# Banded attention of a diffusion backbone: the masks added by TensorE as identity times mask, and the softmax bias taken from a minimum over negated raw scores

## The chip, the cores and the metric

The kernel runs on one core of a Trainium2 chip. The metric is the device time of one execution in microseconds (us), the median of the runs shown. The engines are named as in the profile: PE is TensorE (its weight loads are listed apart as PEld), DVE is VectorE, ACT is ScalarE, POOL is GpSimd, SP is SyncE.

## The reference, cut to what matters

The program is a two-layer backbone over 512 latent tokens and 256 context tokens with 1024 channels. Only one stage of it is changed in its inner loop: the attention of the odd layer. 16 query heads of 64 channels share 4 key heads. A latent query sees all context keys, the latent keys within 128 positions, and one learned logit per head (the sink), all in one softmax:

```python
band = jnp.abs(qi[:, None] + WINDOW - kj[None, :]) <= WINDOW
...
s_loc = jnp.einsum("bqhrd,bkhd->bhrqk", qb, kb).astype(F32) * scale
s_loc = jnp.where(valid, s_loc, -jnp.inf)
s_ctx = jnp.einsum("bqhrd,bkhd->bhrqk", qb, kc).astype(F32) * scale
prob = jax.nn.softmax(jnp.concatenate([s_loc, s_ctx, sink_l], axis=-1), axis=-1).astype(v.dtype)
```

The queries are normalised (root mean square, times a gain vector `q_g`) and rotated before this; `scale` is 1/8.

## The kernel before, in words

The stage works through 32 units: 8 pairs of heads times 4 query tiles of 128 rows. A unit holds two heads (`e` is 0 or 1) whose 64 channels lie in the lower and the upper half of the partitions, so that the score matmuls of the two heads use the upper and the lower 64 rows of the PE array. A unit at either end of the sequence (query tile 0 or 3, an *outer* unit) has 4 key tiles of 128 per head: 2 of context, 2 of its neighbourhood. A unit in the middle (query tile 1 or 2, an *inner* unit) has 5. One key tile per head of an outer unit, and two per head of an inner one, lie on the edge of the band and need a triangular mask. The scores of unit u lie in three of the eight banks of PSUM (the accumulation memory); even and odd units take different banks. Head 0 of an inner unit takes columns 0 to 639 and head 1 columns 896 to 1535, so that key tile (head 0, number 4) and key tile (head 1, number 0) share a bank; the semaphore `wn_tail` makes the matmul of tile (1,0) wait until that of tile (0,4) is done.

Nothing is scheduled by a planner: each engine has its own program, written out as one loop over u, and works it in order.

- PE (`pe_window`), for u: the scores of unit u (L1428, after the exponentials of unit u-2); then the transposes of the probabilities of unit u-2 (L1446), in rounds of up to four tiles through one bank (2 rounds for an outer unit, 3 for an inner one), each round after ACT has copied out the one before; between and behind the rounds the products with the values of unit u-3 (L1470). I call these blocks S, T and V.
- ACT (`act_window`), for u: the copies of the rounds of unit u-2 (L1485); the rounded output of unit u-3 (L1489); then the exponentials of unit u, one for each head with its row sum (L1498), and of the sink (L1502).
- DVE (`dve_window`), for u: mask added in PSUM (L1512), maximum over each head's scores (L1517), then small ones of 128x2: maximum with the sink (L1520), the negated maximum as bias (L1523), sink minus maximum (L1524). Then the sum, reciprocal and normalisation of unit u-1 (L1530 to L1535), and the rest of the output of unit u-3 (L1541).

The two ends of the stage meet the neighbouring products: the value projection (L1204) ahead, the output projection (L498) behind, whose first products are already mixed into the last units. POOL works far from this stage, above all at the start of the program, where it issues loads of modulation weights (L669, L692).

Of the kernel before, what the change touches and what calls it, by code (L numbers as in the profile page):

```python
# [16 lines left out]
F32R = mybir.dt.float32r  # L17

ACT = mybir.ActivationFunctionType
ALU = mybir.AluOpType  # L20
# [30 lines left out]
C_ID, C_ONE, C_BLK, C_UF, C_UB, C_TF, C_TB, C_MP, C_MN, C_SW, C_COS, C_SIN = (  # L51
    0, 128, 256, 384, 512, 640, 768, 896, 1024, 1152, 1280, 1792)
C_ALL = 2304
NEG = -1.0e30


VA_MOD, VA_C, VA_CC, VA_N = 0, 72, 80, 88
# [5 lines left out]
def shape_constants():  # L63

    c = np.zeros((P, C_ALL), np.float32)
    i = np.arange(P)
    c[:, C_ID:C_ID + P] = np.eye(P)
    c[:, C_ONE:C_ONE + P] = 1.0
    c[:, C_BLK:C_BLK + P] = (i[:, None] // 64) == (i[None, :] // 64)
    c[:, C_UF:C_UF + P] = i[:, None] > i[None, :]  # L70
    c[:, C_UB:C_UB + P] = i[:, None] < i[None, :]
    c[:, C_TF:C_TF + P] = i[:, None] <= i[None, :]
    c[:, C_TB:C_TB + P] = i[:, None] >= i[None, :]
    c[:, C_MP:C_MP + P] = np.where(i[None, :] >= i[:, None], 0.0, NEG)
    c[:, C_MN:C_MN + P] = np.where(i[None, :] <= i[:, None], 0.0, NEG)
    swap = np.zeros((P, P), np.float32)
    for o in range(P):
        j = o % 32
        if j < 16:
            swap[o + 16, o] = -1.0  # L80
        else:
            swap[o - 16, o] = 1.0
    c[:, C_SW:C_SW + P] = swap
    quarter = 16
    freqs = (np.float32(10000.0) ** (-np.arange(quarter, dtype=np.float32) / np.float32(quarter))).astype(np.float32)
    t = np.arange(SEQ)
# [34 lines left out]
def build(nc, a, out):  # L121
# [5 lines left out]
    with ExitStack() as ctx:  # L127
# [102 lines left out]
        sink = sb("sink", QH)  # L230
        stat = sb("stat", 32)
        gst = sb("gst", 64)

        def blocks_(x, t=T):
            return x[:, :].rearrange("p (b t) -> p b t", t=t)
# [18 lines left out]
        def c_(at, n=P):  # L254
# [50 lines left out]
        v_mm, v_done, v_done_act = sem("v_mm"), sem("v_done"), sem("v_done_act")  # L305
        at_sc, at_m0, at_nm, at_ex, at_ri, at_pn, at_tr, at_pt, at_pv, at_o = (
            sem("at_" + s) for s in ("sc", "m0", "nm", "ex", "ri", "pn", "tr", "pt", "pv", "o"))
        kk_two, wn_tail = sem("kk_two"), sem("wn_tail")
        wn_sc, wn_mk, wn_mx, wn_m, wn_nm, wn_sk, wn_ex, wn_es, wn_l, wn_ri, wn_n0, wn_n1, wn_tr, wn_pt, wn_pv, wn_hi, wn_lo = (
            sem("wn_" + s) for s in ("sc", "mk", "mx", "m", "nm", "sk", "ex", "es", "l", "ri", "n0", "n1", "tr", "pt", "pv",  # L310
                                     "hi", "lo"))
        pj_ev = sem("pj_ev")
        cv_pad, cv_tap, cv_out = sem("cv_pad"), sem("cv_tap"), sem("cv_out")
# [1057 lines left out]
        for x in range(8):  # L1371
            for qt in range(SEQ // P):
                lo, hi = max(0, qt - 1), min(3, qt + 1)
                if hi - lo == 2:
                    tiles = ([4, 5, qt - 1, qt + 1, qt], [qt, 4, 5, qt - 1, qt + 1])
                    order = [(0, 4, 1), (1, 1, 2), (0, 0, 2), (1, 3, 1), (0, 2, 1), (1, 4, 1), (0, 3, 1), (1, 0, 1)]
                    first, mask = (0, 896), (256, C_MP, 256)
                else:
                    tiles = ([4, 5, lo, hi], [4, 5, lo, hi])
                    order = [(0, 0, 2), (1, 0, 2), (0, 2, 2), (1, 2, 2)]  # L1380
                    first, mask = (0, 1024), ((384, C_MN, P) if qt == 0 else (256, C_MP, P))
                WU.append(dict(x=x, g=x // 2, q0=P * qt, tiles=tiles, order=order, first=first, mask=mask, n=P * len(tiles[0])))
        NWU = len(WU)
        rounds = tails = 0
        for x in WU:
# [4 lines left out]

        def win(u, c0, c1):
            return ps[:, 1536 * (u % 2) + c0:1536 * (u % 2) + c1]

        def pool_keys(pool):

# [16 lines left out]
                    mm.then_inc(w_used, 1)  # L1412

        def pe_window(pe):
            early = [(d, k) for k in range(DB - 1) for d in range(2)]
            for u in range(NWU + 3):
                if u < NWU:
                    x = WU[u]
                    g, q0 = x["g"], x["q0"]
                    if u >= 2:  # L1420
                        pe.wait_ge(wn_ex, 2 * u - 2)
                    for e, j, m in x["order"]:
                        c = x["first"][e] + P * j
                        k0 = P * x["tiles"][e][j]
                        r = slice(64 * e, 64 * e + 64)
                        if x["tail"] and (e, j) == (1, 0):
                            pe.wait_ge(wn_tail, x["tail"])
                        mm = pe.matmul(win(u, c, c + P * m), gq[r, x["x"], q0:q0 + P], gk[r, g, k0:k0 + P * m],  # L1428
                                       start=True, stop=True)
                        if x["tail"] and (e, j) == (0, 4):  # L1430
                            mm.then_inc(wn_tail, 1)
                    mm.then_inc(wn_sc, 1)
                todo = list(range(WU[u - 3]["n"] // P)) if u >= 3 else []
                i = u - 2
                if 0 <= i < NWU:
                    x = WU[i]
                    nt = 2 * x["n"] // P
                    for r in range(x["nr"]):
                        if r == 0:
                            pe.wait_ge(wn_n0, i + 1)  # L1440
                        if 4 * r + 4 > nt // 2 and (r == 0 or 4 * r <= nt // 2):
                            pe.wait_ge(wn_n1, i + 1)
                        if x["r0"] + r:
                            pe.wait_ge(wn_pt, x["r0"] + r)
                        for k in range(4 * r, min(nt, 4 * r + 4)):
                            mm = pe.transpose(bank(6)[:, P * (k % 4):P * (k % 4) + P], gp[:, i % 3, P * k:P * k + P], ident)  # L1446
                        mm.then_inc(wn_tr, 1)
# [27 lines left out]
        def act_window(act):  # L1475
            for u in range(NWU + 3):
# [13 lines left out]
                if u < NWU:  # L1490
# [5 lines left out]
                    for e in range(2):  # L1496
                        c = x["first"][e]
                        act.activation(gp[:, u % 3, n * e:n * e + n], win(u, c, c + n), ACT.Exp,  # L1498
                                       bias=gst[:, u % 4, 2, e:e + 1], scale=HD ** -0.5,
                                       accum_out=gst[:, u % 4, 4, e:e + 1]).then_inc(wn_ex, 1)  # L1500
                    act.wait_ge(wn_sk, u + 1)
                    act.activation(gst[:, u % 4, 5, :], gst[:, u % 4, 3, :], ACT.Exp).then_inc(wn_es, 1)  # L1502

        def dve_window(dve):
            for u in range(NWU + 3):
                if u < NWU:
                    x = WU[u]
                    f = gst[:, u % 4]
                    dve.wait_ge(wn_sc, u + 1)
                    c0, mk, w = x["mask"]  # L1510
                    s = win(u, 0, 1536).rearrange("p (b n) -> p b n", n=512)[:, 0:3:2, c0:c0 + w]
                    dve.tensor_tensor(s, c_(mk, w).rearrange("p (o n) -> p o n", o=1).broadcast_to([P, 2, w]), s,  # L1512
                                      ALU.add).then_inc(wn_mk, 1)
                    dve.wait_ge(wn_mk, u + 1)
                    c = x["first"][1]
                    s = win(u, 0, 2 * c).rearrange("p (b n) -> p b n", n=c)[:, :, 0:x["n"]]
                    dve.tensor_reduce(f[:, 0, :], s, AX, ALU.max).then_inc(wn_mx, 1)  # L1517
                    sk = sink[:, 2 * x["x"]:2 * x["x"] + 2]
                    dve.wait_ge(wn_mx, u + 1)
                    dve.scalar_tensor_tensor(out=f[:, 1, :], in0=f[:, 0, :], scalar=HD ** -0.5, in1=sk,  # L1520
                                             op0=ALU.mult, op1=ALU.max).then_inc(wn_m, 1)
                    dve.wait_ge(wn_m, u + 1)
                    dve.tensor_scalar(f[:, 2, :], f[:, 1, :], -1.0, None, ALU.mult).then_inc(wn_nm, 1)  # L1523
                    dve.tensor_tensor(f[:, 3, :], sk, f[:, 1, :], ALU.subtract).then_inc(wn_sk, 1)  # L1524
                i = u - 1
                if 0 <= i < NWU:
                    f, n = gst[:, i % 4], WU[i]["n"]
# [1222 lines left out]
        def _(act):  # L2750
# [59 lines left out]
            act_norm(act, 3)  # L2810
            act_s_ff(act, 2)
            act_norm(act, 4)
            act_items(act, n_even, len(items), BASE["odd"])
            act_split(act, BASE["out", R_GQA])
            act_v_o(act)
# [95 lines left out]
```

## Time and profile before

| what | value |
|---|---|
| median of 3 runs | 3269.77 us (3262.24 to 3270.68) |
| span of the profiled execution | 3264.5 us |
| PE busy | 3099.5 us, 95% |
| DVE busy | 1924.2 us, 59% |
| ACT busy | 1137.1 us, 35% |
| the attention stage, first scores to last value product | 2693.6 to 2843.7 us |

The profiled execution's span stands for its time; no time of its own is listed beside it, and it lies between the lowest run and the median. Times of day in the rows are microseconds from the start of the span. A busy share of PE counts overlapping matmuls once, so it says when PE had something in flight, not how much of its rate was used.

### The profile page before, as it was taken

The page shows a single profiled execution, that of the slowest core. Times are in us where ns is not written, and L with a number is a line of the kernel's source. Part 1 is how long each engine was busy: PE and PEld are TensorE (multiplying, and loading weights), DVE is VectorE, ACT ScalarE, POOL GpSimd, SP SyncE. Part 2 cuts the span into 40 slices and gives each one's busy share as a digit, 9 for nine tenths or more (in the row PEclk, how much of TensorE's full clock was granted, in tenths as well). Part 3 has the DMA queues.
Part 4 walks back from the last instruction along what each step waited for, and adds up shares of the span by engine and source line. Part 5 has one row for each costly group of instructions (what it writes and reads, how often), then busy time and mean ns, then how long its engine had stood idle before and what let it go on. Part 6 is the DMA issues. An engine that isn't in the chain of part 4 may idle for free.

```text
span 3264.5 us, 43658 instructions
## 1 busy us (share of the span) xinstructions
PE 3099.5 (95%) x17735; PEld 2739.4 (84%) x17735; DVE 1924.2 (59%) x2675; ACT 1137.1 (35%) x1750; POOL 266.0 (8%) x317
## 2 busy tenths in 40 slices
PE   4999999999999998899999999999999998999999
PEld 4999999987669895488999988999998876678887
DVE  7754536424552535767778765877778448643333
ACT  5211212456441321235323334533323536642222
POOL 1100000200001005620000001000000100000000
PEclk8999999999999999999999999999999999999999
DMA  5533424411004220012343321333333120023332
GB/s 205 172 104 104 128 72 137 123 40 52 7 1 124 64 65 14 1 33 78 110 129 104 117 65 59 112 99 106 104 117 118 50 59 8 14 84 97 97 97 90
DMA packets 314303, 274.19 MB, mean 84 GB/s; under 512 B 17426, under 2 KB 290057, under 8 KB 313865
## 3 DMA queue, kind: packets, MB, share of 16 engines
q1 hardware_dynamic: 286992, 182.35, 18.7%
q0 software_dynamic: 25488, 89.14, 8.7%
q8 instruction: 130, 2.13, 0.3%
q14 instruction: 52, 0.43, 0.0%
q10 hardware_dynamic: 1641, 0.14, 0.0%
HBM read 263.21 MB, written 8.39 MB: 83 GB/s over the span
## 4 chain that ended last, share of the span: by engine, by line
PE 52%; DVE 3%; ACT 2%; issue 1%; POOL 0%; ACTq 0%; DVEq 0%
PE ps L2229 30%; PE ps L498 16%; PE ps L1446 1%; ACT gpt L1485 1%; DVE hs_lo L2422 1%; ACT gp L1498 1%; PE ps L1470 1%; PE ps L1428 1%; PE ps L1204 1%; PE ps L2311 0%; DVE vw_lo L2162 0%; PE ps L1884 0%; DVE h_sb L2430 0%; PE ps L1901 0%; DVE ms_s L2453 0%
## 5 line engine op out<-in xcount | busy, mean ns | idle before, releaser
L488 DVE TENSOR_TENSOR w_lo<-ring,w_hi 128x1024 fp32r<-128x1024 f32 (+3 forms) x221 | 251.3, 1138 | 452.4 <-ACT w_hi L473 363.5
L498 PE MATMUL ps<-u_hi,w_hi 128*128 128x384 f32 (+2 forms) x1584 | 468.5, 355 | 22.1 <-DVE u_lo L659 18.0
L498 PE MATMUL ps<-u_hi,w_lo 128*128 128x384 f32 (+2 forms) x1584 | 462.1, 351 | 0.0
L498 PE MATMUL ps<-u_lo,w_hi 128*128 128x384 f32 (+2 forms) x1584 | 462.0, 351 | 0.0
L473 ACT CAST w_hi<-ring 128x1024 fp32r<-128x1024 f32 (+3 forms) x157 | 149.4, 952 | 613.4 <-PE ps L498 574.4
L498 PEld LDWEIGHTS ps<-u_hi,w_hi 128*128 128x128 f32 x1584 | 285.6, 190 | 48.1 <-issue 25.6
L498 PEld LDWEIGHTS ps<-u_lo,w_hi 128*128 128x128 f32 x1584 | 286.7, 190 | 22.7 <-issue 1.7
L498 PEld LDWEIGHTS ps<-u_hi,w_lo 128*128 128x128 f32 x1584 | 285.6, 189 | 21.2
L2156 ACT CAST vw_hi<-ring 128x1024 fp32r<-128x1024 f32 (+1 forms) x176 | 181.2, 1030 | 341.9 <-PE ps L2229 280.7
L2162 DVE TENSOR_TENSOR vw_lo<-ring,vw_hi 128x1024 fp32r<-128x1024 f32 (+1 forms) x176 | 210.9, 1200 | 150.5 <-ACT vw_hi L2156 150.2
L2229 PE MATMUL ps<-u_hi,vw_hi 128*128 128x384 f32 x768 | 248.6, 337 | 12.8 <-DVE u_lo L659 12.3
L2229 PE MATMUL ps<-u_lo,vw_hi 128*128 128x384 f32 x768 | 248.0, 337 | 0.0
L2229 PE MATMUL ps<-u_hi,vw_lo 128*128 128x384 f32 x768 | 247.7, 336 | 0.0
L2229 PE MATMUL ps<-hs_hi,vw_hi 128*128 128x512 f32 x704 | 184.3, 343 | 15.7 <-DVE hs_lo L2422 8.0
L2229 PE MATMUL ps<-hs_hi,vw_lo 128*128 128x512 f32 x704 | 182.7, 341 | 0.0
L2229 PE MATMUL ps<-hs_lo,vw_hi 128*128 128x512 f32 x704 | 181.8, 339 | 0.0
L2229 PE MATMUL ps<-vv_hi,vw_hi 128*128 128x384 f32 x480 | 161.9, 337 | 0.0
L2453 DVE SCALAR_TENSOR_TENSOR ms_s<-cst,sc,ms_s 128x1024 f32<-128x1024 f32 x126 | 158.4, 1280 | 5.1 <-DVE ms_s L2453 0.5
L2229 PE MATMUL ps<-vv_hi,vw_lo 128*128 128x384 f32 x480 | 161.2, 336 | 0.0
L2229 PE MATMUL ps<-vv_lo,vw_hi 128*128 128x384 f32 x480 | 161.1, 336 | 0.0
L498 PE MATMUL ps<-hid_hi,w_hi 128*128 128x384 f32 (+1 forms) x528 | 159.5, 356 | 0.0
L498 PE MATMUL ps<-hid_hi,w_lo 128*128 128x384 f32 (+1 forms) x528 | 159.1, 355 | 0.0
(351 smaller groups left out, 5871.3 us busy)
## 6 DMA issues: line engine op xcount, KB each, us to landing
ring<-in_w_ff_in SPq DMA_DIRECT2D x176, 512.0 KB, 3.9
ring<-in_w_ff_out SPq DMA_DIRECT2D x72, 512.0 KB, 4.0
cst<-in_w_mod POOLq DMA_DIRECT2D x72, 512.0 KB, 3.9
m_in<-in_w_mod POOLq DMA_DIRECT2D x56, 512.0 KB, 4.0
ring<-in_w_in_e SPq DMA_DIRECT2D x26, 512.0 KB, 3.9
m_first<-in_w_mod POOLq DMA_DIRECT2D x16, 512.0 KB, 13.9
ring<-in_w_out_e SPq DMA_DIRECT2D x16, 512.0 KB, 3.8
ring<-in_w_ff_out SPq DMA_DIRECT2D x16, 384.0 KB, 3.4
```

The lines of the kernel that those rows point to most:

```text
L473: act.copy(w_hi[:, (n % 2) * SLOT:(n % 2) * SLOT + WIDE[n]], ring[:, (n % RING) * SLOT:(n % RING) * SLOT + WIDE[n]]).then_inc(w_split_hi, 1)
L488: dve.tensor_tensor(w_lo[:, b:b + WIDE[n]], ring[:, s:s + WIDE[n]], w_hi[:, b:b + WIDE[n]], ALU.subtract).then_inc(w_split_lo, 1)
L498: mm = pe.matmul(ps_at(p, c0, c1) if halved else pair(p)[:, c0:c1], w, x[:, c0:c1], start=start and i == 0, stop=stop and i == 2)
L1204: mm = pe.matmul(out, x, w[:, b:b + m], start=start and i == 0, stop=stop and i == 2)
L1428: mm = pe.matmul(win(u, c, c + P * m), gq[r, x["x"], q0:q0 + P], gk[r, g, k0:k0 + P * m], start=True, stop=True)
L1446: mm = pe.transpose(bank(6)[:, P * (k % 4):P * (k % 4) + P], gp[:, i % 3, P * k:P * k + P], ident)
L1470: mm = pe.matmul(bank(7)[64 * e:64 * e + 64, 0:P], gv[:, k, HD * y["g"]:HD * y["g"] + HD], gpt[:, u % 2, c:c + P], start=j == 0, stop=j == ...
L1485: act.copy(gpt[:, i % 2, c0:c1], bank(6)[:, 0:c1 - c0]).then_inc(wn_pt, 1)
L2156: act.copy(v_hi_w[c % 3][:, 0:src.shape[-1]], src).then_inc(c_hi, 1)
L2162: dve.tensor_tensor(v_lo_w[c % 3][:, 0:n], src, v_hi_w[c % 3][:, 0:n], ALU.subtract).then_inc(c_lo, 1)
L2229: mm = pe.matmul(y, w, x[:, c0:c1], start=start and i == 0, stop=stop and i == 2, skip_group_check=onto)
L2453: y = dve.scalar_tensor_tensor(out=at_, in0=w, scalar=by, in1=at_, op0=ALU.mult, op1=ALU.add)
```

## The change

Four edits belong together. The scale of 1/8 and a minus sign are multiplied into the gain vector of the query norm, and the sink is negated, both once, early, by POOL; the scores then come out of PE as minus the scaled logits. The masks hold plus 1e30 in place of minus 1e30 and are no longer added by DVE: two matmuls of PE per unit (128x128 identity times two blocks of 128 mask columns, one of them all zeros for an outer unit) write them into PSUM ahead of the scores, and the score matmuls of those key tiles add to them. The order of the score matmuls of a unit is changed, so that the masked tiles come first; for an inner unit this puts tile (0,4) next to last and tile (1,0) last. DVE takes a minimum where it took a maximum, and the minimum with the negated sink is the bias itself; the exponential runs with scale -1.

```diff
-                    order = [(0, 4, 1), (1, 1, 2), (0, 0, 2), (1, 3, 1), (0, 2, 1), (1, 4, 1), (0, 3, 1), (1, 0, 1)]
-                    first, mask = (0, 896), (256, C_MP, 256)
+                    order = [(0, 2, 1), (1, 3, 1), (0, 3, 1), (1, 4, 1), (0, 0, 2), (1, 1, 2), (0, 4, 1), (1, 0, 1)]
+                    first, masked, mask = (0, 896), ((2, 3), (3, 4)), wm[:, P:4 * P].rearrange("p (b n) -> p b n", n=P)[:, 0:3:2, :]
...
-                    order = [(0, 0, 2), (1, 0, 2), (0, 2, 2), (1, 2, 2)]
+                    order = [(0, 2, 2), (1, 2, 2), (0, 0, 2), (1, 0, 2)]
...
+        def pool_masks(pool):
+
+            pool.wait_ge(const_in, 16)
+            pool.tensor_copy(wm[:, 0:P], ident).then_inc(wm_made, 1)
+            pool.tensor_copy(wm[:, P:2 * P], c_(C_MP)).then_inc(wm_made, 1)
+            pool.tensor_scalar(wm[:, 2 * P:3 * P], ident, 0.0, None, ALU.mult).then_inc(wm_made, 1)
+            pool.tensor_copy(wm[:, 3 * P:4 * P], c_(C_MN)).then_inc(wm_made, 1)
+            pool.wait_ge(vec_done, 3)
+            pool.tensor_scalar(sink[:, :], sink[:, :], -1.0, None, ALU.mult).then_inc(turned, 1)
+            pool.tensor_scalar(vb[:, VB_GQ:VB_GQ + 1], vb[:, VB_GQ:VB_GQ + 1], -HD ** -0.5, None, ALU.mult).then_inc(turned, 1)
...
+            pe.wait_ge(wm_made, 4)
...
+                    for e in range(2):
+                        c = 1024 * e + 256
+                        pe.matmul(win(u, c, c + 256).rearrange("p (b n) -> p b n", n=P), wm[:, 0:P], x["mask"],
+                                  start=True, stop=False, skip_group_check=True)
...
-                                       start=True, stop=True)
+                                       start=j not in x["masked"][e], stop=True, skip_group_check=True)
...
-                                       bias=gst[:, u % 4, 2, e:e + 1], scale=HD ** -0.5,
+                                       bias=gst[:, u % 4, 2, e:e + 1], scale=-1.0,
...
+            dve.wait_ge(turned, 2)
...
-                    dve.tensor_tensor(s, c_(mk, w).rearrange("p (o n) -> p o n", o=1).broadcast_to([P, 2, w]), s,
-                                      ALU.add).then_inc(wn_mk, 1)
-                    dve.wait_ge(wn_mk, u + 1)
...
-                    dve.tensor_reduce(f[:, 0, :], s, AX, ALU.max).then_inc(wn_mx, 1)
+                    dve.tensor_reduce(f[:, 0, :], s, AX, ALU.min).then_inc(wn_mx, 1)
...
-                    dve.scalar_tensor_tensor(out=f[:, 1, :], in0=f[:, 0, :], scalar=HD ** -0.5, in1=sk,
-                                             op0=ALU.mult, op1=ALU.max).then_inc(wn_m, 1)
-                    dve.wait_ge(wn_m, u + 1)
-                    dve.tensor_scalar(f[:, 2, :], f[:, 1, :], -1.0, None, ALU.mult).then_inc(wn_nm, 1)
-                    dve.tensor_tensor(f[:, 3, :], sk, f[:, 1, :], ALU.subtract).then_inc(wn_sk, 1)
+                    dve.tensor_tensor(f[:, 2, :], f[:, 0, :], sk, ALU.min).then_inc(wn_nm, 1)
+                    dve.wait_ge(wn_nm, u + 1)
+                    dve.tensor_tensor(f[:, 3, :], f[:, 2, :], sk, ALU.subtract).then_inc(wn_sk, 1)
```

ACT also gets a wait for `turned` ahead of the odd layer's projections, and `pool_masks` stands between POOL's first loads (L669) and its next (L692).

On PE, around the scores of one inner unit, before: the last value product of an earlier unit, then six groups of score matmuls (`gk` keys, `gq` queries, `ps` PSUM), then the first transposes (`gp` probabilities, `cst` the identity).

```order
L1470 MATMUL ps<-gpt,gv 64x128 x2
L1428 MATMUL ps<-gk,gq 128x128 [waits wn_ex]
L1428 MATMUL ps<-gk,gq 128x256 x2
L1428 MATMUL ps<-gk,gq 128x128 x4
L1428 MATMUL ps<-gk,gq 128x128 [waits wn_tail]
L1446 MATMUL ps<-cst,gp 128x128 [waits wn_pt,wn_n0]
L1446 MATMUL ps<-cst,gp 128x128 x3
```

The first score row there is tile (0,4), seven matmuls ahead of the one that waits for it. The same place after the change, with the two mask matmuls (`wm`):

```order
L1489 MATMUL ps<-gpt,gv 64x128 x2
L1439 MATMUL ps<-wm 128x256 [waits wn_ex]
L1439 MATMUL ps<-wm 128x256
L1447 MATMUL ps<-gk,gq 128x128 x4
L1447 MATMUL ps<-gk,gq 128x256 x2
L1447 MATMUL ps<-gk,gq 128x128
L1447 MATMUL ps<-gk,gq 128x128 [waits wn_tail]
L1465 MATMUL ps<-cst,gp 128x128 [waits wn_pt,wn_n0]
L1465 MATMUL ps<-cst,gp 128x128 x3
```

The two mask matmuls stand between the value products and the scores and take over the wait for the exponentials, and the matmul that waits for `wn_tail` now directly follows the one that signals it. On DVE, one unit before (`gst` holds the small vectors):

```order
L1512 TENSOR_TENSOR ps<-cst,ps 128x2x128 [waits wn_sc]
L1517 TENSOR_REDUCE gst<-ps 128x2 [waits wn_mk]
L1520 SCALAR_TENSOR_TENSOR gst<-gst,sink 128x2 [waits wn_mx]
L1523 TENSOR_SCALAR gst<-gst 128x2 [waits wn_m]
L1524 TENSOR_TENSOR gst<-sink,gst 128x2
L1530 TENSOR_TENSOR gst<-gst 128x2 [waits wn_es,wn_ex]
L1532 RECIPROCAL gst<-gst 128x2 [waits wn_l]
L1534 TENSOR_SCALAR gp<-gp,gst 128x640 [waits wn_ri]
L1535 TENSOR_SCALAR gp<-gp,gst 128x640
L1541 TENSOR_TENSOR go_lo<-ps,go_hi 128x128 [waits wn_hi]
```

And after:

```order
L1532 TENSOR_REDUCE gst<-ps 128x2 [waits wn_sc]
L1535 TENSOR_TENSOR gst<-gst,sink 128x2 [waits wn_mx]
L1537 TENSOR_TENSOR gst<-gst,sink 128x2 [waits wn_nm]
L1543 TENSOR_TENSOR gst<-gst 128x2 [waits wn_es,wn_ex]
L1545 RECIPROCAL gst<-gst 128x2 [waits wn_l]
L1547 TENSOR_SCALAR gp<-gp,gst 128x640 [waits wn_ri]
L1548 TENSOR_SCALAR gp<-gp,gst 128x640
L1554 TENSOR_TENSOR go_lo<-ps,go_hi 128x128 [waits wn_hi]
```

Two of ten instructions of DVE are gone, the mask and one of the small ones, and the reduction waits for PE's scores directly.

## Rows read from the trace of the kernel before

**Rows 1.** The page, busy time: engine, us (share of the span) xinstructions

```profile
PE 3099.5 (95%) x17735; PEld 2739.4 (84%) x17735; DVE 1924.2 (59%) x2675; ACT 1137.1 (35%) x1750; POOL 266.0 (8%) x317
```

**Rows 2.** One stretch: length, busy (count) of PE PEld DVE ACT POOL, clock, DMA

```profile
2740.00:2760.00 20.00, 18.58 (x182) 12.98 (x179) 17.61 (x49) 14.94 (x42) 0.00 (x0) 1.00 0.00 1
```

**Rows 3.** Waits, 2720 to 2820: waiter, whom for, us, times, longest

```profile
ACT gpt L1485 <- PE ps L1446: 26.0, 41, 0.8
...
PEld ps L1446 <- DVE gp L1534: 2.4, 6, 0.4
```

**Rows 4.** Groups by form, 2720 to 2820: count, busy us, mean ns, idle before

```profile
L1498 ACT ACTIVATE gp<-ps,gst 128x640 f32<-128x640 f32 x24 | 18.9, 797 | 0.1
...
L1428 PE MATMUL ps<-gk,gq 64*128 64x128 f32 x141 | 15.2, 279 | 0.0
...
L1512 DVE TENSOR_TENSOR ps<-cst,ps 128x512 f32<-128x512 f32 x12 | 8.3, 696 | 4.4 <-PE ps L1428 4.3
...
L1512 DVE TENSOR_TENSOR ps<-cst,ps 128x256 f32<-128x256 f32 x12 | 5.1, 424 | 1.2 <-PE ps L1428 1.2
...
L1523 DVE TENSOR_SCALAR gst<-gst 128x2 f32<-128x2 f32 x23 | 3.9, 169 | 0.8
```

**Rows 5.** Timeline, one round of four units: start, duration, what, idle before

```profile
2753.29 1.37 PE L1428 MATMUL ps<-gk,gq 64*128 64x128 f32 x16
2754.59 0.66 PE L1446 MATMUL ps<-cst,gp 128*128 128x128 f32 x4
2755.28 0.58 ACT L1485 COPY gpt<-ps 128x512 f32<-128x512 f32 x1
...
2757.16 1.13 PE L1428 MATMUL ps<-gk,gq 64*128 64x256 f32 x8
...
2759.08 0.59 ACT L1485 COPY gpt<-ps 128x512 f32<-128x512 f32 x1
...
2761.12 0.44 PE L1446 MATMUL ps<-cst,gp 128*128 128x128 f32 x2
...
2761.49 1.13 PE L1428 MATMUL ps<-gk,gq 64*128 64x256 f32 x8
...
2762.56 0.66 PE L1446 MATMUL ps<-cst,gp 128*128 128x128 f32 x4
...
2763.14 0.66 PE L1470 MATMUL ps<-gpt,gv 128*64 128x128 f32 x8
2763.45 0.60 ACT L1485 COPY gpt<-ps 128x512 f32<-128x512 f32 x1
...
2766.24 1.37 PE L1428 MATMUL ps<-gk,gq 64*128 64x128 f32 x16
...
2768.23 0.59 ACT L1485 COPY gpt<-ps 128x512 f32<-128x512 f32 x1 [0.17 <-PE ps L1446]
...
2770.33 1.37 PE L1428 MATMUL ps<-gk,gq 64*128 64x128 f32 x16
```

**Rows 6.** Timeline of PE, the value projection: 256 columns, single-pass type

```profile
2692.49 0.28 PE L1204 MATMUL ps<-w_lo,u_hi 128*128 128x256 f32 x1
2692.61 0.28 PE L1204 MATMUL ps<-w_hi,u_hi 128*128 128x256 f32 x1
```

**Rows 7.** Timeline and one stretch (columns as in Rows 2) at the stage's start

```profile
2695.66 0.42 DVE L1512 TENSOR_TENSOR ps<-cst,ps 128x256 f32<-128x256 f32 x1
...
2699.27 2.51 PE L1428 MATMUL ps<-gk,gq 64*128 64x128 f32 x16 [3.40 <-ACT gp L1498]
...
2710.26 1.14 PE L1428 MATMUL ps<-gk,gq 64*128 64x256 f32 x8
...
2698.00:2700.00 2.00, 0.73 (x5) 0.73 (x7) 1.93 (x3) 1.31 (x5) 0.00 (x0) 0.53 0.00 0
```

**Rows 8.** Timeline near the program's start: ACT's last gain copy, POOL's loads

```profile
45.61 0.20 ACT L2790 COPY vc<-ps 128x60 f32<-128x60 f32 x1
...
74.57 1.05 POOL L692 DMA_DIRECT2D m_in<-in_w_mod  x2 [43.81 <-DVE u_lo L659]
```

More of the change, by code:

```diff
@@ L53 @@
 C_ALL = 2304
-NEG = -1.0e30
+FAR = 1.0e30
 VA_MOD, VA_C, VA_CC, VA_N = 0, 72, 80, 88
@@ L73, in shape_constants @@
     c[:, C_TB:C_TB + P] = i[:, None] >= i[None, :]
-    c[:, C_MP:C_MP + P] = np.where(i[None, :] >= i[:, None], 0.0, NEG)
-    c[:, C_MN:C_MN + P] = np.where(i[None, :] <= i[:, None], 0.0, NEG)
+    c[:, C_MP:C_MP + P] = np.where(i[None, :] >= i[:, None], 0.0, FAR)
+    c[:, C_MN:C_MN + P] = np.where(i[None, :] <= i[:, None], 0.0, FAR)
     swap = np.zeros((P, P), np.float32)
@@ L232, in build @@
         gst = sb("gst", 64)
+        wm = ctx.enter_context(nc.sbuf_tensor("wm", [P, 4 * P], F32R))
         def blocks_(x, t=T):
@@ L307, in build @@
             sem("at_" + s) for s in ("sc", "m0", "nm", "ex", "ri", "pn", "tr", "pt", "pv", "o"))
-        kk_two, wn_tail = sem("kk_two"), sem("wn_tail")
-        wn_sc, wn_mk, wn_mx, wn_m, wn_nm, wn_sk, wn_ex, wn_es, wn_l, wn_ri, wn_n0, wn_n1, wn_tr, wn_pt, wn_pv, wn_hi, wn_lo = (
-            sem("wn_" + s) for s in ("sc", "mk", "mx", "m", "nm", "sk", "ex", "es", "l", "ri", "n0", "n1", "tr", "pt", "pv",
+        kk_two, wn_tail, wm_made, turned = sem("kk_two"), sem("wn_tail"), sem("wm_made"), sem("turned")
+        wn_sc, wn_mx, wn_nm, wn_sk, wn_ex, wn_es, wn_l, wn_ri, wn_n0, wn_n1, wn_tr, wn_pt, wn_pv, wn_hi, wn_lo = (
+            sem("wn_" + s) for s in ("sc", "mx", "nm", "sk", "ex", "es", "l", "ri", "n0", "n1", "tr", "pt", "pv",
                                      "hi", "lo"))
@@ L1375, in build @@
                     tiles = ([4, 5, qt - 1, qt + 1, qt], [qt, 4, 5, qt - 1, qt + 1])
-                    order = [(0, 4, 1), (1, 1, 2), (0, 0, 2), (1, 3, 1), (0, 2, 1), (1, 4, 1), (0, 3, 1), (1, 0, 1)]
-                    first, mask = (0, 896), (256, C_MP, 256)
+                    order = [(0, 2, 1), (1, 3, 1), (0, 3, 1), (1, 4, 1), (0, 0, 2), (1, 1, 2), (0, 4, 1), (1, 0, 1)]
+                    first, masked, mask = (0, 896), ((2, 3), (3, 4)), wm[:, P:4 * P].rearrange("p (b n) -> p b n", n=P)[:, 0:3:2, :]
                 else:
                     tiles = ([4, 5, lo, hi], [4, 5, lo, hi])
-                    order = [(0, 0, 2), (1, 0, 2), (0, 2, 2), (1, 2, 2)]
-                    first, mask = (0, 1024), ((384, C_MN, P) if qt == 0 else (256, C_MP, P))
-                WU.append(dict(x=x, g=x // 2, q0=P * qt, tiles=tiles, order=order, first=first, mask=mask, n=P * len(tiles[0])))
+                    order = [(0, 2, 2), (1, 2, 2), (0, 0, 2), (1, 0, 2)]
+                    first, masked = (0, 1024), ((2,), (2,))
+                    mask = (wm[:, 2 * P:4 * P] if qt == 0 else wm[:, P:3 * P]).rearrange("p (b n) -> p b n", n=P)
+                WU.append(dict(x=x, g=x // 2, q0=P * qt, tiles=tiles, order=order, first=first, masked=masked, mask=mask,
+                               n=P * len(tiles[0])))
         NWU = len(WU)
@@ L1509, in dve_window @@
                     dve.wait_ge(wn_sc, u + 1)
-                    c0, mk, w = x["mask"]
-                    s = win(u, 0, 1536).rearrange("p (b n) -> p b n", n=512)[:, 0:3:2, c0:c0 + w]
-                    dve.tensor_tensor(s, c_(mk, w).rearrange("p (o n) -> p o n", o=1).broadcast_to([P, 2, w]), s,
-                                      ALU.add).then_inc(wn_mk, 1)
-                    dve.wait_ge(wn_mk, u + 1)
                     c = x["first"][1]
                     s = win(u, 0, 2 * c).rearrange("p (b n) -> p b n", n=c)[:, :, 0:x["n"]]
-                    dve.tensor_reduce(f[:, 0, :], s, AX, ALU.max).then_inc(wn_mx, 1)
+                    dve.tensor_reduce(f[:, 0, :], s, AX, ALU.min).then_inc(wn_mx, 1)
                     sk = sink[:, 2 * x["x"]:2 * x["x"] + 2]
                     dve.wait_ge(wn_mx, u + 1)
-                    dve.scalar_tensor_tensor(out=f[:, 1, :], in0=f[:, 0, :], scalar=HD ** -0.5, in1=sk,
-                                             op0=ALU.mult, op1=ALU.max).then_inc(wn_m, 1)
-                    dve.wait_ge(wn_m, u + 1)
-                    dve.tensor_scalar(f[:, 2, :], f[:, 1, :], -1.0, None, ALU.mult).then_inc(wn_nm, 1)
-                    dve.tensor_tensor(f[:, 3, :], sk, f[:, 1, :], ALU.subtract).then_inc(wn_sk, 1)
+                    dve.tensor_tensor(f[:, 2, :], f[:, 0, :], sk, ALU.min).then_inc(wn_nm, 1)
+                    dve.wait_ge(wn_nm, u + 1)
+                    dve.tensor_tensor(f[:, 3, :], f[:, 2, :], sk, ALU.subtract).then_inc(wn_sk, 1)
                 i = u - 1
@@ L2812, in _ @@
             act_norm(act, 4)
+            act.wait_ge(turned, 2)
             act_items(act, n_even, len(items), BASE["odd"])
@@ L2871, in _ @@
             pool_mod_first(pool)
+            pool_masks(pool)
             for part in PARTS:
```

## The prediction

> **What bounds the kernel now.** The page's busy times come first: PE is in flight for 95% of the span, DVE for 59% [rows 1]. That is an average over many stages, so the next view is the stage of the change alone, cut into stretches. There PE is in flight for 18.58 of 20 us, DVE busy for 17.61, ACT for 14.94 [rows 2]. DVE looks almost as full as PE, and an edit that takes work from DVE looks right. Busy time does not say who waits for whom, so the list of waits is third: in 100 us PE's weight loads waited for DVE 2.4 us in 6 places, while ACT's copies waited for PE's transposes 26.0 us in 41 [rows 3]. ACT itself hardly ever waited before an exponential (0.1 us for 24 of them), so DVE's maximum always comes early enough [rows 4].
>
> The timeline then shows the loop. A round of four units lasts from 2753.29 to 2770.33, 17.04 us [rows 5], and the 32 units are eight such rounds. Call its four steps by their score blocks: a (inner, 2753.29), b (outer, 2757.16), c (outer, 2761.49), d (inner, 2766.24). Each step begins with S, PE's scores. Two things then run side by side: on PE the scores S and the first transposes T; on ACT the output of an older unit and the exponentials of the unit before. Both must be over before ACT's first copy can start, and everything later in the step hangs on that copy. Measured from the start of S it starts at 1.99 (a), 1.92 (b), 1.96 (c), 1.99 us (d) [rows 5].
>
> PE's side of this: an inner S lasts 1.30 us to the first transposes (2753.29 to 2754.59), these 0.66, and the copy follows 0.03 later: 1.99. So a and d are bounded by PE (in d the copy's row names PE as what it waited for); in a ACT ends at the same time, since its row shows no idle time. An outer S lasts 1.07 (2761.49 to 2762.56), so PE would be ready at 1.07 + 0.69 = 1.76, and in b and c ACT ends last, PE with 0.16 and 0.20 us to spare.
>
> **The change part by part.** *Taken from DVE:* the mask, 0.696 us in an inner and 0.424 in an outer unit, and one small instruction, 0.169 [rows 4]; with the hand-overs some 0.75 us a unit, 24 us over 32. Of this the loop gets back only what waits for DVE, 0.1 us a unit by the 2.4 us in 24 units [rows 3], and those waits lie in b, where ACT ends later anyhow. I take 0, with 3.2 us (32 x 0.1) as the other bound. Only the first unit's chain is exposed: there PE waits 3.40 us for the first exponentials [rows 7], and DVE's mask (0.42) and the small one (0.17) stand ahead of them: gain 0.6 us.
>
> *Added to PE, masks.* Two matmuls of 256 columns in the single-pass type. The value projection has this shape, and its matmuls follow each other 0.12 us apart [rows 6]: 0.24 us. Then the price of one more kind of block. Two transposes hold PE for 0.37 us (2761.12 to 2761.49), four for 0.58 (2762.56 to 2763.14) [rows 5]: 0.11 each and 0.15 for the block as such. The mask block stands between V, which uses the array in column halves, and S, which uses it in row halves. I take 0.24 + 0.15 = 0.39 us for each unit. Bounds: 0.24 if the block costs nothing by itself; 0.47 with 0.23, which is what an inner S of 1.30 has above its 1.07 of streaming (ten key tiles, five in each half; four outer tiles of twice the width last 1.07 with the same edge, so 0.21 each).
> The Trainium skill bears on the 0.15: TensorEngine Tiling (Array Packing), section Key Properties, says that changing the tiling mode, not merely the tile, drains TensorE. The trace agrees with 0.15 us for each block. The Trainium skill's page TensorE: Matmul & The Clock Gate, section Back-to-back issue gap, lists 262 cycles for 256 columns, an estimate of 0.22 us for the two masks with nothing on top; by that figure the sum would come out near the third case below.
>
> *Added to PE, the order of the scores.* Tile (1,0) has to wait for tile (0,4). Before, the two stood at the ends of the block; now they are neighbours [the order rows above]. Streaming, five tiles of a half take 1.07; the last record of (0,4) starts 0.11 before that and lasts 0.28 [rows 4], so it is done at 1.24; the release takes 0.03 to 0.11, and (1,0) then streams alone for 0.21: 1.48 to 1.56 in place of 1.07. I take 0.45 us for each inner unit. Bounds: 0.21, only the lost overlap, or 0 if the wait were hidden; 0.6 with the largest of each. With the masks an inner S grows by 0.84, an outer one by 0.39.
>
> *The sum.* In a and d PE ends last already, so the whole 0.84 lands in each. In b PE is ready at 1.76 + 0.39 = 2.15 against 1.92: 0.23. In c 2.15 against 1.96: 0.19. A round gains 0.84 + 0.84 + 0.23 + 0.19 = 2.10 us, eight rounds 16.8. The first two units' scores are hidden under the wait for the first exponentials: minus 0.19 + 0.84. Minus 0.6 at the start. Sum: +15.2 us. Against the profiled 3264.5 us this is 0.46%; the profile lies 5.3 below the median, and I add the 15 us to the median: **3285 us**.
>
> *Costed at nothing.* POOL's four copies, two small ones and their wait for the gains stand in an idle stretch of 43.81 us ahead of its load at 74.57, and the gains are there by 45.8 [rows 8]; without that cover a load of modulation weights would start late by their length, under 1 us estimated from their small size. The waits for `turned` and `wm_made` are met some 2600 us earlier. Exponentials with another scale and a minimum for a maximum keep their shapes.
>
> *PE's clock.* At the stage's start PE has waited 3.40 us and the granted clock falls to 0.53, the lower of its levels of 1.2 and 2.4 GHz; the two steps from 2699.27 to 2710.26 last 10.99 us [rows 7], against 8.20 in the round (2753.29 to 2761.49). The masks lengthen PE's work ahead of this gap by 1.2 us and the shorter DVE chain ends it 0.6 earlier. If the clock stays up, 2.8 us come back; if it falls again, the masks of two steps cost double, 1 us more. I take neither, and keep both for the range.
>
> **Rivals.**
> (1) *PE is the bound and pays for masks and order*, as above: +10 to +20 us, 3280 to 3290.
> (2) *DVE is the bound.* It is busy for 88% of the stage, and in inner units its next mask follows its last instruction closely. If PE and ACT waited for it, 24 us would come back, with the masks on PE in its shadow: 3246 us. It decides if the exponentials wait for the bias; 0.1 us for 24 of them speaks against it.
> (3) *PE pays little:* the masks stream at 0.12 us with no cost as a block, and the wait for tile (0,4) is mostly hidden. Inner S +0.24 to +0.45, outer +0.24: a round gains 0.24 x 2 + 0.08 + 0.04 = 0.60 up to 1.02, eight rounds 4.8 to 8.2, less 1: +4 to +7 us, 3274 to 3277, with the clock's 2.8 back +1. The 0.12 of rows 6 speaks for it; the 0.15 of every block in rows 5 against.
> (4) *PE pays more:* the identity's weights cannot be loaded while row halves are in use, on either side of the block, or the mask's two separate pieces of PSUM write slowly. 0.2 us more for each unit is 6.4, with the upper bounds (0.47 and 0.6: 2.72 a round, 21.8, less 1.9) +20 to +27: 3290 to 3297.
>
> **How the numbers follow.** Measured runs of this kernel differ by 0.25%, so about 0.3%, 9.8 us, tells from no change. Chances: (1) 0.58, (2) 0.04, (3) 0.26, (4) 0.12. Faster: case (2), 0.04. Slower: (4) and nearly all of (1), 0.68. Same: (3) and the low edge of (1), 0.28. The range leaves out (2), the top of (4) and the very bottom of (3): 3269 to 3293 us.
>
> **What would show it.** Right: the round grows from 17.04 to about 19.1 us; an inner S with its masks lasts about 2.1 us to the next transposes and an outer one 1.46; in every step ACT's first copy names PE as what it waited for; DVE's busy share of the stage falls from 88 to some 63% (3.75 us a unit less 0.75, over 4.79), with more waiting for PE's scores. Wrong: inner and outer S grow by the same 0.24 (no cost of a block, no wait), or the round gets shorter, or a gap opens in PE's record ahead of tile (1,0) that is far from 0.2 to 0.3 us, or the difference lies outside the stage.

## The result, and the profile after

The changed kernel takes 3283.17 us, the median of 6 runs (3275.34 to 3286.39). The kernel before takes 3263.76 us in the median of its 6 runs (3262.24 to 3270.68). The ratio is 1.0048 with a 95% interval of 1.0038 to 1.0058, so the change costs 15.7 us of 3264 (12.4 to 18.9). The means of the six runs each lie as far apart (3281.03 and 3265.49), the medians 19.4 us. The profiled execution of the changed kernel took 3275.34 us, with a span of 3273.5 us; it is the shortest of the six and has the highest mean granted clock, 0.985 against 0.980 to 0.983 in the others.

The page's busy times come first, then the stage cut as in [rows 2] (length; busy and count of PE, PEld, DVE, ACT, POOL; clock; DMA share and GB/s), both of the changed kernel:

```profile
PE 3109.5 (95%) x17799; PEld 2745.2 (84%) x17799; DVE 1907.9 (58%) x2611; ACT 1139.4 (35%) x1750; POOL 271.0 (8%) x323
```

```profile
2698.00:2700.00 2.00, 1.46 (x12) 1.31 (x14) 1.86 (x7) 1.19 (x3) 0.00 (x0) 1.00 0.00 0
...
2740.00:2760.00 20.00, 18.81 (x174) 13.23 (x171) 13.26 (x35) 12.93 (x35) 0.00 (x0) 1.00 0.00 1
```

In the second of these stretches DVE is relieved as planned: 13.26 us of 20 busy in place of 17.61. ACT is less busy too, 12.93 for 14.94, though its work is the same: the stage itself has become slower. PE is in flight as much as before. Over one whole round of four units, which 20 us is not, DVE is busy for 12.58 of 19.25 us (65%) where it was 14.79 of 17.04 (87%), and ACT for 12.51 where it was 12.32. The list of waits of the changed kernel from 2730 to 2830 (waiter, whom for, us in total, times, longest) shows where the slack went:

```profile
ACT gpt L1504 <- PE ps L1465: 33.7, 43, 1.1
DVE gst L1532 <- PE ps L1447: 23.9, 21, 1.7
...
PEld ps L1447 <- PE ps L1447: 2.5, 10, 0.2
```

Before, DVE kept PE's weight loads waiting 2.4 us in 100 [rows 3]; that line is gone. DVE now waits 23.9 us for PE's scores (its mask waited 5.4 for them before), ACT's copies wait 33.7 us for PE's transposes where it was 26.0, and a new line has appeared, in which PE waits for itself, 0.25 us in each inner unit. The timeline of one round shows the steps (start, duration, engine, line, shapes, count, idle time before; L1439 are the masks, L1447 the scores, L1465 the transposes, L1504 ACT's copies):

```profile
2741.87 0.44 PE L1465 MATMUL ps<-cst,gp 128*128 128x128 f32 x2
2742.06 0.48 PE L1439 MATMUL ps<-wm 128*128 128x256 f32 x2
...
2742.47 1.14 PE L1447 MATMUL ps<-gk,gq 64*128 64x256 f32 x8
...
2743.54 0.66 PE L1465 MATMUL ps<-cst,gp 128*128 128x128 f32 x4
...
2744.23 0.59 ACT L1504 COPY gpt<-ps 128x512 f32<-128x512 f32 x1
...
2747.00 0.50 PE L1439 MATMUL ps<-wm 128*128 128x256 f32 x2
...
2747.43 1.17 PEld L1447 LDWEIGHTS ps<-gk,gq 64*128 64x128 f32 x14
2747.44 1.91 PE L1447 MATMUL ps<-gk,gq 64*128 64x128 f32 x16
...
2748.86 0.29 PEld L1447 LDWEIGHTS ps<-gk,gq 64*128 64x128 f32 x2 [0.25 <-PE ps L1447]
...
2749.27 0.66 PE L1465 MATMUL ps<-cst,gp 128*128 128x128 f32 x4
...
2749.97 0.59 ACT L1504 COPY gpt<-ps 128x512 f32<-128x512 f32 x1 [1.14 <-PE ps L1465]
...
2752.06 0.50 PE L1439 MATMUL ps<-wm 128*128 128x256 f32 x2
...
2755.02 0.59 ACT L1504 COPY gpt<-ps 128x512 f32<-128x512 f32 x1 [0.92 <-PE ps L1465]
...
2756.89 0.50 PE L1439 MATMUL ps<-wm 128*128 128x256 f32 x2
...
2759.08 0.59 ACT L1504 COPY gpt<-ps 128x512 f32<-128x512 f32 x1
...
2761.31 0.48 PE L1439 MATMUL ps<-wm 128*128 128x256 f32 x2
```

From mask to mask of the same step (2742.06 to 2761.31) a round lasts 19.25 us; it was 17.04 [rows 5]. From a step's first mask to its first score it is 0.43 to 0.44 us (2747.00 to 2747.44; 0.41 where transposes stand ahead, 2742.06 to 2742.47). Inner scores take 1.83 us to the next transposes (2747.44 to 2749.27) where they took 1.30; outer ones take 1.07 (2742.47 to 2743.54) as before. ACT's first copy starts 2.96 us into the inner steps (2752.06 to 2755.02) and names PE with an idle time of about a microsecond; in the outer steps it starts 2.17 and 2.19 us in, where it was 1.96 and 1.92, and names nobody. The weight loads (PEld) of the inner block show what made its scores longer: fourteen of sixteen run through, then tile (1,0) waits 0.25 us for tile (0,4), PE for PE.

The start of the stage went the other way. First the changed kernel, then two rows of the kernel before that were not shown yet, its first scores and its last value products:

```profile
2689.88 0.47 PE L1439 MATMUL ps<-wm 128*128 128x256 f32 x2 [0.51 <-issue]
...
2694.85 0.50 PE L1439 MATMUL ps<-wm 128*128 128x256 f32 x2 [1.16 <-ACT gp L1517]
...
2703.98 1.14 PE L1447 MATMUL ps<-gk,gq 64*128 64x256 f32 x8
...
2851.47 1.09 PE L1489 MATMUL ps<-gpt,gv 128*64 128x128 f32 x16
```

```profile
2693.64 2.23 PE L1428 MATMUL ps<-gk,gq 64*128 64x256 f32 x24 [0.51 <-issue]
...
2842.63 1.09 PE L1470 MATMUL ps<-gpt,gv 128*64 128x128 f32 x16
```

PE waits 1.16 us for the first exponentials where it waited 3.40 [rows 7], and the granted clock stays at 1.00 all through the start of the stage, as in the stretch from 2698 to 2700 above, where it had fallen to 0.53. From the stage's first instruction on PE to the scores of the fifth unit it is 14.10 us (2689.88 to 2703.98); before, 16.62 (2693.64 to 2710.26). Over all, first instruction to last value products, the stage takes 161.59 us against 148.99: 12.6 us more. From the fifth unit on it is 15.12 of these (147.49 for 132.37); seven rounds of 2.21 would be 15.47. The stage's 12.6 lies within the interval of the whole time, 12.4 to 18.9. Outside the stage the two traces differ the other way: the spans by 9.0 us (3273.5 and 3264.5), so the rest of the program was 3.6 us shorter in the changed kernel's, and e5_moved below, with the same products on PE ahead of the stage, reaches it at 2686.93 where the kernel before does at 2693.64. One trace of each cannot tell where the other 3 us of the 15.7 come from.

### The profile page after: what moved, and what is told of

The parts are those of the page before. It is cut to its first block, busy times and chain, and to the rows that moved or that the text cites. A ratio compares the mean times of both kernels' runs of the same rounds, so it can differ in the third digit from the quotient of the medians.

```text
span 3273.5 us, 43729 instructions
## 1 busy us (share of the span) xinstructions
PE 3109.5 (95%) x17799; PEld 2745.2 (84%) x17799; DVE 1907.9 (58%) x2611; ACT 1139.4 (35%) x1750; POOL 271.0 (8%) x323
## 4 chain that ended last, share of the span: by engine, by line
PE 52%; DVE 3%; ACT 2%; issue 1%; POOL 0%; ACTq 0%; DVEq 0%
PE ps L2242 29%; PE ps L499 16%; PE ps L1465 1%; PE ps L1447 1%; ACT gpt L1504 1%; DVE hs_lo L2435 1%; PE ps L1205 1%; PE ps L2324 0%; PE ps L1489 0%; DVE vw_lo L2175 0%; ACT gp L1517 0%; DVE ms_s L2466 0%; DVE h_sb L2443 0%; PE ps L1897 0%; PE ps L1914 0%
## 5 line engine op out<-in xcount | busy, mean ns | idle before, releaser
L499 PE MATMUL ps<-hid_lo,w_hi 128*128 128x384 f32 (+1 forms) x528 | 158.5, 354 | 0.0
```

What stands on the lines that cost most here:

```text
L499: mm = pe.matmul(ps_at(p, c0, c1) if halved else pair(p)[:, c0:c1], w, x[:, c0:c1], start=start and i == 0, stop=stop and i == 2)
```

## The experiments

Six more kernels were run. The whole time carries several microseconds of spread (35 runs of the kernel before, taken beside e1, e3, e5 and e7, went from 3258.66 to 3273.01 us), while the round of four units repeats to 0.01 us within most of a trace; the exception behind the start is one step some 40 us into the stage, 0.11 us longer in the kernel before, e2 and e3, and 0.05 in e5. So the round, read where that step is not in it, is what each verdict goes by, and the ratio says whether the whole agrees. The round is read from the score blocks of one trace, from one unit to the one of the same kind four units on.

| kernel | round us | inner scores to transposes | mask block | ratio to before, 95% |
|---|---|---|---|---|
| before | 17.04 | 1.30 | none | 1 |
| the change | 19.25 | 1.83 | 0.43 | 1.0048 (1.0038 to 1.0058) |
| e1_order | 18.19 | 1.30 | 0.43 | 1.0013 (1.0002 to 1.0023) |
| e7_tail | 18.12 | 1.83 | none | 1.0023 (1.0013 to 1.0033) |
| e3_nomask | 17.04 | 1.30 | none | 0.9998 (0.9988 to 1.0008) |
| e5_moved | 17.16 | 1.30 | elsewhere | 0.9988 (0.9977 to 0.9999) |
| e6_double | 20.20 | 1.84 | 0.67 | 1.0054 (1.0037 to 1.0070) |
| e2_fold | 17.04 | 1.30 | none | 0.9997 (0.9987 to 1.0006) |

**e1_order: the wait taken away.** Against the change:

```diff
-                    order = [(0, 2, 1), (1, 3, 1), (0, 3, 1), (1, 4, 1), (0, 0, 2), (1, 1, 2), (0, 4, 1), (1, 0, 1)]
+                    order = [(0, 4, 1), (1, 3, 1), (0, 2, 1), (1, 4, 1), (0, 3, 1), (1, 1, 2), (0, 0, 2), (1, 0, 1)]
```

Tile (0,4) lies in a bank of its own half, so it may go first without touching the masks. Expected:

> The change with the scores of an inner unit in another order: tile (0,4) first again, then the masked tiles, the context tiles, tile (1,0) last, so that (1,0) no longer follows the tile it waits for. Theory A (PE pays for the mask block and, in inner units, for the wait of a tile on its direct predecessor): inner scores to first transposes 1.30 us in place of 1.84, outer ones 1.07 as they are, the round of four units 19.25 - 2 x 0.54 = 18.2 us, 8.6 us less than the change, 7 us above before (ratio about 1.002). Theory B (masks and accumulation on top of them make the scores slow, the order costs nothing): inner scores stay near 1.8, round 19.2, ratio 1.0048.

Its timeline on PE, two outer units four apart and an inner one:

```profile
2738.50 1.13 PE L1447 MATMUL ps<-gk,gq 64*128 64x256 f32 x8
...
2743.03 0.51 PE L1439 MATMUL ps<-wm 128*128 128x256 f32 x2
...
2743.46 1.37 PE L1447 MATMUL ps<-gk,gq 64*128 64x128 f32 x16
...
2744.76 0.66 PE L1465 MATMUL ps<-cst,gp 128*128 128x128 f32 x4
...
2756.69 1.13 PE L1447 MATMUL ps<-gk,gq 64*128 64x256 f32 x8
```

Inner scores are back at 1.30 us (2743.46 to 2744.76), the mask block ahead of them is still 0.43, and the round is 18.19. The order alone costs 19.25 - 18.19 = 1.06 us a round, about half of the loss. Accumulating on masks already in PSUM costs nothing: the score block has its old length. Theory B falls.

**e7_tail: the wait alone.** The kernel before with the change's order of scores:

```diff
-                    order = [(0, 4, 1), (1, 1, 2), (0, 0, 2), (1, 3, 1), (0, 2, 1), (1, 4, 1), (0, 3, 1), (1, 0, 1)]
+                    order = [(0, 2, 1), (1, 3, 1), (0, 3, 1), (1, 4, 1), (0, 0, 2), (1, 1, 2), (0, 4, 1), (1, 0, 1)]
```

> The kernel before with nothing but the changed order of the scores of inner units; masks stay on DVE. Theory A: inner scores 1.84 us in place of 1.30, round 17.04 + 2 x 0.54 = 18.1 us, 8.6 us more than before, ratio 1.0026. Theory B: round 17.0, ratio 1.000.

```profile
2741.16 1.13 PE L1428 MATMUL ps<-gk,gq 64*128 64x256 f32 x8
...
2750.25 1.91 PE L1428 MATMUL ps<-gk,gq 64*128 64x128 f32 x16
2751.67 0.29 PEld L1428 LDWEIGHTS ps<-gk,gq 64*128 64x128 f32 x2 [0.25 <-PE ps L1428]
2752.08 0.42 PEld L1446 LDWEIGHTS ps<-cst,gp 128*128 128x128 f32 x4
...
2759.28 1.14 PE L1428 MATMUL ps<-gk,gq 64*128 64x256 f32 x8
```

The same 0.25 us of PE waiting for PE, inner scores of 1.83 us (2750.25 to 2752.08), a round of 18.12: 1.08 us more, with no mask on PE at all. The two halves of the loss are independent of each other: 1.08 here and 1.15 in e1 (18.19 - 17.04) add up to 2.23, and the change costs 2.21.

**e3_nomask: DVE without its mask, PE as before.** Keys outside the band take part in this kernel's softmax. Against the change, besides the old order:

```diff
-                    for e in range(2):
-                        c = 1024 * e + 256
-                        pe.matmul(win(u, c, c + 256).rearrange("p (b n) -> p b n", n=P), wm[:, 0:P], x["mask"],
-                                  start=True, stop=False, skip_group_check=True)
...
-                                       start=j not in x["masked"][e], stop=True, skip_group_check=True)
+                                       start=True, stop=True)
```

> The change with the masks left out altogether (neither DVE nor PE adds one; keys outside the band take part in the softmax) and the old order of the scores, so PE does what it did before and DVE is without its mask. Theory A (DVE's mask was covered): round 17.0 us as before, only the start of the stage shorter by 0.6 us, or by some 3 us more if the clock stays at its upper level there: ratio 0.9990 to 1.000. Rival (DVE bounded the stage): 0.75 us less for each unit, round 14.0 us, 24 us less, ratio 0.993.

```profile
2690.80 2.23 PE L1443 MATMUL ps<-gk,gq 64*128 64x256 f32 x24 [0.51 <-issue]
2695.76 1.37 PE L1443 MATMUL ps<-gk,gq 64*128 64x128 f32 x16 [2.73 <-ACT gp L1513]
2697.07 0.66 PE L1461 MATMUL ps<-cst,gp 128*128 128x128 f32 x4
...
2737.88 1.14 PE L1443 MATMUL ps<-gk,gq 64*128 64x256 f32 x8
...
2754.92 1.14 PE L1443 MATMUL ps<-gk,gq 64*128 64x256 f32 x8
...
2836.05 1.09 PE L1485 MATMUL ps<-gpt,gv 128*64 128x128 f32 x16
```

The round is 17.04 us (2737.88 to 2754.92), the same to the hundredth as with the masks on DVE. All of DVE's mask work in the loop was covered, and the rival that expected a round of 14.0 falls. What the relief can give is at the start: the stage takes 145.25 us (2690.80 to 2836.05), 3.7 less than before, and the clock stays up in this execution: four transposes at 2697.07 take their usual 0.66 us. The whole time's interval, -3.9 to +2.6 us, holds that but cannot show it.

**e2_fold: the scale, sign and minimum alone.** Masks stay on DVE; of the change's small instructions this kernel has:

```diff
-                    dve.tensor_reduce(f[:, 0, :], s, AX, ALU.max).then_inc(wn_mx, 1)
+                    dve.tensor_reduce(f[:, 0, :], s, AX, ALU.min).then_inc(wn_mx, 1)
...
-                    dve.tensor_scalar(f[:, 2, :], f[:, 1, :], -1.0, None, ALU.mult).then_inc(wn_nm, 1)
-                    dve.tensor_tensor(f[:, 3, :], sk, f[:, 1, :], ALU.subtract).then_inc(wn_sk, 1)
+                    dve.tensor_tensor(f[:, 2, :], f[:, 0, :], sk, ALU.min).then_inc(wn_nm, 1)
+                    dve.wait_ge(wn_nm, u + 1)
+                    dve.tensor_tensor(f[:, 3, :], f[:, 2, :], sk, ALU.subtract).then_inc(wn_sk, 1)
```

> The kernel before with the scale, the sign and the minimum alone: masks are added by DVE as before (plus 1e30 in place of minus 1e30), one small DVE instruction less for each unit, PE unchanged. Theory A: round 17.0 us as before, the start of the stage 0.2 us shorter, ratio 1.000. Rival (DVE bounded the stage): 0.2 us less for each unit, 6.4 us, ratio 0.998. [...]

```profile
2698.97 1.37 PE L1437 MATMUL ps<-gk,gq 64*128 64x128 f32 x16 [3.20 <-ACT gp L1507]
2701.01 1.11 PE L1455 MATMUL ps<-cst,gp 128*128 128x128 f32 x4 [0.67 <-DVE gp L1542]
```

The first wait is 0.20 us shorter (3.20 for 3.40), the round 17.04 and the ratio 0.9997 with 1 well inside. These edits are free and worth nothing that this measurement can tell. The clock fell here as before, though not at once: transposes of four tiles still take 1.11 us at 2701.01, where 0.66 is their usual length.

**e6_double: the masks twice.** The masked logits get 2e30, which ends in the same zero:

```diff
-                    for e in range(2):
-                        c = 1024 * e + 256
-                        pe.matmul(win(u, c, c + 256).rearrange("p (b n) -> p b n", n=P), wm[:, 0:P], x["mask"],
-                                  start=True, stop=False, skip_group_check=True)
+                    for t in range(2):
+                        for e in range(2):
+                            c = 1024 * e + 256
+                            pe.matmul(win(u, c, c + 256).rearrange("p (b n) -> p b n", n=P), wm[:, 0:P], x["mask"],
+                                      start=t == 0, stop=False, skip_group_check=True)
```

> The change with each mask matmul issued twice (the masked scores get plus 2e30 in place of 1e30, which the exponential turns into the same zero). Theory A (a mask matmul of 256 columns streams in 0.12 us, and the rest of the block's 0.43 is the price of the block): 0.24 us more in each step, 0.67 from the first mask to the first score, round 19.25 + 4 x 0.24 = 20.2 us, 7.7 us above the change, ratio about 1.007. Rival (each mask matmul costs 0.21 by itself, there is no price of the block): 0.43 more in each step, block 0.86, round 21.0, 13.8 us above the change, ratio 1.009.

```profile
2741.16 0.74 PE L1440 MATMUL ps<-wm 128*128 128x256 f32 x4
...
2741.83 1.91 PE L1448 MATMUL ps<-gk,gq 64*128 64x128 f32 x16
```

Four masks take 0.67 us to the first score, two took 0.43: 0.12 each, and 0.19 for the block as such. The round is 20.20 us, 0.95 more than the change for 4 x 0.24. The rival's 0.86 and 21.0 fall. The whole time came out at 1.0054, below the 1.007 expected, which is the upper end of its interval (1.0037 to 1.0070); it does not tell this kernel from the change, and the 0.95 us a round rests on the trace.

**e5_moved: the masks where PE waits anyway.** The order of e1, and the masks of unit u+1 one step earlier, behind the first value products of step u:

```diff
+        def pe_masks(pe, u):
+            for e in range(2):
+                c = 1024 * e + 256
+                pe.matmul(win(u, c, c + 256).rearrange("p (b n) -> p b n", n=P), wm[:, 0:P], WU[u]["mask"],
+                          start=True, stop=False, skip_group_check=True)
...
+                        if r == 0 and u + 1 < NWU:
+                            pe.wait_ge(wn_ex, 2 * u)
+                            pe_masks(pe, u + 1)
```

> The order of e1, and the two mask matmuls of unit u+1 issued one step earlier, behind the first value products of step u, where PE waits for ACT's copy (0.2 to 0.4 us in the trace of before). Theory A: the masks lie in that wait, their block costs next to nothing (0 to 0.2 us a step): round 17.0 to 17.6 us, and the shorter DVE chain at the start stays as a gain of 1 to 4 us: ratio 0.999 to 1.001. If a mask block costs its 0.42 us wherever it stands: round 18.2 and ratio 1.002 as e1.

```profile
2686.93 0.71 PE L1431 MATMUL ps<-wm 128*128 128x256 f32 x4 [0.51 <-issue]
...
2739.38 1.37 PE L1453 MATMUL ps<-gk,gq 64*128 64x128 f32 x16
...
2741.37 0.59 ACT L1513 COPY gpt<-ps 128x512 f32<-128x512 f32 x1 [0.17 <-PE ps L1471]
2741.85 0.51 PE L1431 MATMUL ps<-wm 128*128 128x256 f32 x2
2742.19 0.60 PE L1471 MATMUL ps<-cst,gp 128*128 128x128 f32 x4
...
2756.54 1.37 PE L1453 MATMUL ps<-gk,gq 64*128 64x128 f32 x16
...
2833.43 1.09 PE L1498 MATMUL ps<-gpt,gv 128*64 128x128 f32 x16
```

The masks run while ACT copies (2741.37 to 2741.96), and the next transposes start 0.23 us behind that copy where it is 0.14 without a mask between (2750.56 to 2750.70 in the changed kernel). The round is 17.16 us (2739.38 to 2756.54), 0.12 more than before, and the stage 146.50 (2686.93 to 2833.43), 2.5 less than before, because the shorter start is kept. The ratio is 0.9988 with an interval that ends just under 1: this version beats the change clearly, and the kernel before by some 4 us, barely shown by the whole time. Its loop still loses 0.12 us a round; the 2.5 us of its stage are no more than the clock's 2.8 at the start, which is read from one execution of each.

## Why the prediction was right

**What bounds the loop.** PE's scores and transposes against ACT's exponentials, with DVE aside, was right, and e3 shows it without any cost on PE: DVE is busy for 12.57 us a round in place of 14.79, 0.55 less a unit (0.75 was counted with the hand-overs), and the round is unchanged at 17.04. The busy shares of 88% and 93% alone would not have told this; the row with 0.1 us of waiting ahead of 24 exponentials did.

**The mask block.** Taken at 0.24 + 0.15 = 0.39, it measured 0.43: 0.24 as predicted, by e6, and 0.19 for the block, within the bounds of 0 and 0.23. That the block has a price is shown; what in the switch of the array takes the time is not.

**The order.** Taken at 0.45, it measured 0.53 to 0.54 in three readings (the change's inner scores, e7's round, and the change's round less e1's), within 0.21 to 0.6 and above the 0.41 to 0.49 that its working gave (1.48 to 1.56 less 1.07). Of the release in that working, 0.03 is in [rows 5]; no row shown gives the 0.11. That PE would wait 0.2 to 0.3 us for itself was right: 0.25.

**Where it lands.** Predicted were 0.84 in each inner step and 0.23 and 0.19 in the outer ones; measured by ACT's first copy, 0.97 and 0.97 (2.96 and 2.97 for 1.99) and 0.27 and 0.21. That would be 2.42 a round and is 2.21, near the 2.10 predicted: 0.2 us come back in a place the prediction did not see. Where a step ends with transposes, the mask follows them after 0.19 us (2741.87 to 2742.06), while the scores had followed after 0.37 [rows 5]: between transposes and masks the block's price is not paid. Both use the whole array (128*128 in their rows), which would account for it; no run tests that. e1's round agrees: 17.04 + 2 x 0.43 + 0.27 + 0.21 - 0.18 = 18.20, measured 18.19. One reading was off without effect: in b the transposes stood 1.14 us behind the scores, not 1.07, since PE waited for DVE there (2757.16 to 2758.30 in the trace of before), so PE had 0.09 us to spare and not 0.16.

**The signs.** The round, the added length of both kinds of scores and PE's wait ahead of tile (1,0) came as forecast, and DVE's share of the round is 65% where some 63% was expected. One sign came only in part: ACT's first copy was to name PE in every step, and it does so in the inner ones (1.14 and 0.92 us of idle time). In the outer ones PE ends last by little: the transposes of 2743.54 end at 2744.20 and the copy starts at 2744.23, with no idle time in its row.

**The start.** The gain of 0.6 us and the two units' scores hidden under the first wait are there. The clock's 2.8 us, which I left out of the sum and kept for the range, came back in the profiled execution: for it, this is the term that was decided the wrong way. With it the sum for the stage is 15.2 - 2.8 = 12.4, and 12.6 is measured. Whether the clock stayed up at the start in the other five executions, whose mean clock is lower, no trace shows.

**The whole.** 3285 against 3283.17 us is closer than the reasoning deserves. The forecast added 15 us to a median of 3269.77; with more runs that median is 3263.76, and the difference of the medians is 19.4 us, that of the ratio 15.7 (12.4 to 18.9). The sum of 15.2 agrees with the ratio; the stage of the one trace shows 12.6 of it. The other 3 us stay open: they can be the spread outside the stage, or a clock at the start that fell in the executions without a trace. That 15.2 and 15.7 agree so closely is therefore in part luck; the round, 2.21 for 2.10, is what the prediction earned. The range was said to leave out the very bottom of (3); that case, at +1 to +7, lies wholly above 3269.

**Costed at nothing.** POOL's work was covered, but its length was underestimated. The changed kernel's POOL rows, the first two and the last of the six small instructions and the load behind them:

```profile
30.75 0.68 POOL L1400 CAST wm<-cst 128x128 fp32r<-128x128 f32 x1
31.39 1.37 POOL L1401 CAST wm<-cst 128x128 fp32r<-128x128 f32 x1
...
46.53 0.22 POOL L1406 TENSOR_SCALAR vb<-vb 128x1 f32<-128x1 f32 x1
74.47 1.13 POOL L693 DMA_DIRECT2D m_in<-in_w_mod  x2 [27.72 <-DVE u_lo L660]
```

The six take 5.95 us in all, not under 1; that estimate had no row behind it. They end at 46.75 with 27.72 us of cover left.

## What to carry to other kernels

An engine's share of busy time does not say that work taken from it is worth anything: look at who waits ahead of the instruction that would come earlier, and if it is nobody, the gain is nothing. Work moved to the engine that ends last is paid in full, here with 0.19 us for each block on top of its streaming; the same work moved into a wait of that engine (e5) cost 0.12 us a round in place of 1.15. When an edit reorders a block, look for pairs that wait for each other inside it: two score tiles that share a bank cost half of this loss because they became neighbours, and putting them apart again took all of that half away.

## What was not expected

- The price of a block depends on its neighbours: 0.19 us between value products and masks and on to the scores, near 0 between transposes and masks.
- PE's wait ahead of the third unit's scores and the clock after it, one execution of each kernel: after waits of 3.40, 3.20 and 2.89 us (before, e2, e7) the granted clock was 0.5 for some microseconds; after 2.73, 2.10, 1.70, 1.16 and 0.69 us (e3, e5, e1, the change, e6) it stayed at 1.0. One execution each does not show that it always does so.
- The spread of the whole time goes with the mean granted clock: of the 35 runs of the kernel before, the shortest, 3258.66 us, has 0.984 and the longest, 3273.01 us, 0.980. Where in the program the clock differed, runs without a trace do not say.
- The four 128x128 instructions with a change of type took POOL 0.68 to 1.40 us each.
